# Joining the tokens after layer 0: latents first, with PE doing the sum, and layer 1's queries ahead of the context

## The reference, cut to what matters

```
for l in range(2):
    h = modulate(rms_norm(x, norm1_g), shift, scale)      # the same for ctx with its own shift, scale
    y_lat, y_ctx = parallel_mixer(h_lat, h_ctx, w_in[l], ...)
    x, ctx = x + g1 * y_lat, ctx + cg1 * y_ctx
    f = grouped_moe(concat(h2_ctx, h2_lat), ...)          # per token: w0 * expert_a + w1 * expert_b
    ctx, x = ctx + cg2 * f[:, :256], x + g2 * f[:, 256:]
return rms_norm(x, final_g)                               # layer 1 leaves the context's output out
```

## Time and profile before

| | |
|---|---|
| median of 3 runs | 1466.73 us (1465.39 to 1467.75) |
| profiled execution, first to last instruction | 1467.6 us (the page gives no other time for it) |
| PE busy | 1403.9 us, 96% |
| DVE, ACT, POOL busy | 695.9, 527.6, 157.1 us |
| mean granted clock of TensorE | 0.988 |
| DMA moved | 352.37 MB, mean 240 GB/s |
| PE in slices 23 to 25 (843.9 to 953.9 us) | 8 or 9 tenths and more |

### The profile page before, as it was taken

One profiled execution on the slowest core, in us unless ns is written; L12 is line 12 of the kernel. 1 busy time (PEld: TensorE's weight loads), 2 busy tenths in 40 slices (PEclk: granted clock), 3 DMA queues, 4 the chain that ended last, 5 costly groups with the idle time before them and its releaser, 6 DMA issues. The chain is left out here.

```text
span 1467.6 us, 20788 instructions
## 1 busy us (share of the span) xinstructions
PE 1403.9 (96%) x8454; PEld 899.7 (61%) x8454; DVE 695.9 (47%) x1201; ACT 527.6 (36%) x955; POOL 157.1 (11%) x163
## 2 busy tenths in 40 slices
PE   4999999999999999999999979999998999999997
PEld 2787667646888864444444478876856997344433
DVE  3477986475834442100000035877675864223323
ACT  4554452357233341111111136544346453112112
POOL 0006970000000000000000030074000000000000
PEclk9999999999999999999999989999999999999999
DMA  9862104671131757999999592121577765999994
GB/s 355 250 153 92 53 6 172 229 287 59 58 115 58 286 203 290 374 389 396 402 397 411 226 330 83 58 72 44 200 258 289 284 232 230 387 427 428 427 427 167
DMA packets 102952, 352.37 MB, mean 240 GB/s; under 512 B 23104, under 2 KB 26304, under 8 KB 88000
## 3 DMA queue, kind: packets, MB, share of 16 engines
q1 hardware_dynamic: 99136, 338.09, 60.3%
q0 software_dynamic: 2976, 10.49, 2.1%
q10 hardware_dynamic: 736, 2.36, 0.4%
HBM read 341.48 MB, written 13.63 MB: 242 GB/s over the span
## 5 line engine op out<-in xcount | busy, mean ns | idle before, releaser
L1471 PE MATMUL bank<-narrow_slab,picked 128*64 128x512 f32 x256 | 114.7, 601 | 4.4 <-issue 4.2
L1202 PE MATMUL bank<-slab,feed 128*64 128x512 f32 x512 | 115.8, 605 | 0.2 <-issue 0.2
L1472 PE MATMUL bank<-narrow_slab,picked 128*64 128x512 f32 x256 | 114.7, 601 | 0.0
L864 PE MATMUL bank<-hT,ring 128*128 128x512 f32 (+1 forms) x256 | 102.8, 539 | 0.0
L3101 DVE TENSOR_TENSOR f_acts<-bank,f_silu 64x512 f32<-64x512 f32 x16 | 12.2, 764 | 188.8 <-ACT f_silu L2232 188.8
L1202 PEld LDWEIGHTS bank<-slab,feed 128*64 128x64 f32 x512 | 36.6, 139 | 71.9 <-issue 71.9
L1471 PEld LDWEIGHTS bank<-narrow_slab,picked 128*64 128x64 f32 x256 | 34.1, 138 | 70.2 <-issue 68.8
L2499 POOL DMA_INDIRECT feed_rows<-token_table,slot_token x16 | 14.6, 914 | 555.9 <-DVE slot_token L3033 346.4
L3280 DVE TENSOR_TENSOR hidden<-bank,gated 64x512 f32<-64x512 f32 x16 | 17.4, 1086 | 109.7 <-ACT gated L2374 109.7
L864 PEld LDWEIGHTS bank<-hT,ring 128*128 128x128 f32 x256 | 45.9, 191 | 32.0 <-issue 30.6
L1231 PE MATMUL bank<-slab,f_turned 128*64 128x512 f32 x256 | 58.5, 598 | 0.6 <-issue 0.6
(11 more groups left out here) (421 smaller groups left out, 3025.1 us busy)
## 6 DMA issues: line engine op xcount, KB each, us to landing
ring<-in_w_in SPq DMA_DIRECT2D x23, 2048.0 KB, 11.3
ring<-in_w_ada SPq DMA_DIRECT2D x16, 2048.0 KB, 11.1
slab<-in_w_gate SPq DMA_DIRECT2D x16, 2048.0 KB, 14.8
slab<-in_w_up SPq DMA_DIRECT2D x16, 2048.0 KB, 18.8
slab<-in_w_down SPq DMA_DIRECT2D x16, 2048.0 KB, 19.4
narrow_slab<-in_w_gate SPq DMA_DIRECT2D x16, 2048.0 KB, 15.5
narrow_slab<-in_w_up SPq DMA_DIRECT2D x15, 2048.0 KB, 20.9
narrow_slab<-in_w_down SPq DMA_DIRECT2D x15, 2048.0 KB, 24.6
```

The lines of the kernel that those rows point to most:

```text
L864: mm = T.matmul(beside[0][:, a:TOK], w[:, k, c * P:(c + 1) * P], hT[:, k, a:TOK], start=(k == 0), stop=(k == KT - 1))
L1202: mm = T.matmul(bank[e % 2][NEAR * kind:NEAR * (kind + 1), :], feed[e % 2][:, k, 0:NEAR], w[kind][:, k, :], start=(k == 0), stop=(k == KT ...
L1471: T.matmul(bank[0][0:64, :], x, gate[:, k, :], start=(k == 0), stop=(k == KT - 1))
L1472: mm = T.matmul(bank[0][64:128, :], x, up[:, k, :], start=(k == 0), stop=(k == KT - 1))
```

## The change

The gathers go in the order t = 2, 3, 0, 1 (latents first). The early load of `w_in` block 3 is taken out of its place; SP issues it after the gathers of the first three tiles have landed, and block 4 after the fourth. PE runs 24 idle products in place of 40. A new tile `share_diag` holds for each token tile and each of the two rows a diagonal 128x128 matrix of the shares, made by one multiplication on DVE. PE multiplies the gathered rows by it, so that the scaling, the sum of the two rows and the transposition are one group of 16 products a tile; ACT's scaling, DVE's sum and the transposes go.

The segments are then handled one after the other. PE joins tiles 2, 3 and 0, sums the latents' squares, spreads the latents' factor, and joins tile 1. DVE adds the latents, and then interleaves the latents' norm products with adding the context. PE multiplies the queries by feature tile as soon as the modulated latents are there; behind the third of eight tiles stand the sums of the context's squares, behind the fourth the spread of its factor. The context's squares are made by POOL (five) and DVE (three) in place of ACT, and are not paired. Rounded copies and remainders are made by segment, and the chunks wait for both.

```diff
-        PAIRED = 12
+        JOIN_ORDER = (2, 3, 0, 1)
+        BY_POOL = 5
...
+            def join_squares(sg):
+                key = ("ms", 1, 0) if sg == 0 else ("ms", 1, 0, 1)
+                o = open_bank(key, "norm_std", side=(sg == 0), at=4)
+                for k in range(KT):
...
+                    for t in range(2):
+                        mm = T.matmul(o[:, t:t + 1], square_late[:, KT * sg + k, t * P:(t + 1) * P], ones[:, 0:1],
+                                      start=(k == 0 and t == 0), stop=(k == KT - 1 and t == 1))
...
+            def spread_segment(sg):
...
+                if sg == 1:
+                    idle_products(o[:, 0:P], 2)
+                pe.wait_ge(sem["rstd_found"], stds_before(2) + 2 - sg)
...
+                def join(t):
+                    pe.wait_ge(sem["shares_ready"], 1)
+                    pe.wait_ge(sem[f"tok_there{t}"], 32)
+                    for d in range(KT):
+                        c = d % 2 * SEG + t % 2 * P
+                        for j in range(2):
+                            mm = T.matmul(bank[t // 2 * 4 + d // 2][:, c:c + P], tok_rows[j][:, t, d * P:(d + 1) * P],
+                                          share_diag[:, t, j, :], start=(j == 0), stop=(j == 1))
+                    mm.then_inc(sem["tok_turned"], 1)
...
+                for t in JOIN_ORDER[:3]:
+                    join(t)
+                join_squares(1)
+                spread_segment(1)
+                join(JOIN_ORDER[3])
...
+            def latent_queries():
...
+                for k in range(KT):
+                    pe.wait_ge(sem["h_ready"], normed_before(2) + k + 1)
+                    for c in range(4):
+                        o = bank[6 + c // 2][:, c % 2 * SEG:(c % 2 + 1) * SEG]
+                        mm = T.matmul(o, w[:, k, c * P:(c + 1) * P], hT[:, k, SEG:TOK],
...
+                    if k == 2:
+                        join_squares(0)
+                    if k == 3:
+                        spread_segment(0)
...
-                    idle_products(bank[7][:, P:2 * P], 40)
+                    idle_products(bank[7][:, P:2 * P], 24)
...
-                    fill(first_after[first_lane])
...
-                        for t in range(4):
-                            sp.wait_ge(sem[f"tok_there{t}"], 32)
-                        for s in (4, 5, 6):
+                        for s, before in ((3, JOIN_ORDER[:3]), (4, JOIN_ORDER[3:]), (5, ()), (6, ())):
+                            for t in before:
+                                sp.wait_ge(sem[f"tok_there{t}"], 32)
                             fill(slot_of(("in", 1, s)))
```

ACT in layer 1, where `modulate` over all 512 tokens and the copies behind it stood:

```diff
+                def latents_then_context():
+                    modulate(2, SEG, gain1[:, 1], mod[:, 1, 0:KT, :])
+                    for k in range(KT):
+                        act.wait_ge(sem["h_ready"], normed_before(2) + k + 1)
+                        S.activation(early_hi[:, k, SEG:TOK], hT[:, k, SEG:TOK], ACT.Copy).then_inc(sem["tile_high"], 1)
+                    segment_std(0)
+                    for k in range(KT):
+                        act.wait_ge(sem["normed_ready"], normed_before(2) + KT + k + 1)
+                        S.activation(hT[:, k, 0:SEG], normed[:, k % 2, 0:SEG], ACT.Identity, scale=gain1[:, 1, k, 1:2],
+                                     bias=mod[:, 1, k, 1:2]).then_inc(sem["h_ready"], 1)
+                        act.wait_ge(sem["h_ready"], normed_before(2) + KT + k + 1)
+                        S.activation(early_hi[:, k, 0:SEG], hT[:, k, 0:SEG], ACT.Copy).then_inc(sem["tile_high"], 1)
+                        if k == 3:
+                            near_high(0)
+                    near_high(1)
```

POOL, in place of the pairwise additions of squares:

```diff
+                for k in range(BY_POOL):
+                    if k == 0:
+                        pool.wait_ge(sem["normed_ready"], normed_before(2) + 1)
+                    pool.wait_ge(sem["tok_added"], KT + k + 1)
+                    G.tensor_tensor(square_late[:, k, :], xT[:, k, 0:SEG], xT[:, k, 0:SEG], ALU.mult)\
+                        .then_inc(sem["square_ready"], 1)
```

DVE in layer 1, in place of the norm over all tokens and the remainders behind it:

```diff
+                def latents_then_context():
+                    invert_segment(1)
+                    dve.wait_ge(*is_ready(("rstd", 2)))
+                    rstd = result(("rstd", 2))
+                    for k in range(KT):
+                        if k >= 2:
+                            add_joined(0, k - 2)
+                            dve.wait_ge(sem["h_ready"], normed_before(2) + k - 1)
+                        V.tensor_tensor(normed[:, k % 2, SEG:TOK], xT[:, k, SEG:TOK], rstd[:, SEG:TOK], ALU.mult)\
+                         .then_inc(sem["normed_ready"], 1)
+                    add_joined(0, KT - 2)
+                    add_joined(0, KT - 1)
+                    for k in range(BY_POOL, KT):
+                        dve.wait_ge(sem["tok_added"], KT + k + 1)
+                        V.tensor_tensor(square_late[:, k, :], xT[:, k, 0:SEG], xT[:, k, 0:SEG], ALU.mult)\
+                         .then_inc(sem["square_added"], 1)
+                    for k in range(4):
+                        latent_low(k)
+                    invert_segment(0)
...
+                    for k in range(KT):
...
+                        V.tensor_tensor(normed[:, k % 2, 0:SEG], xT[:, k, 0:SEG], rstd[:, 0:SEG], ALU.mult)\
+                         .then_inc(sem["normed_ready"], 1)
+                        if k < 4:
+                            latent_low(4 + k)
+                        if k:
+                            context_low(k - 1)
+                        if k == 4:
+                            near_low(0)
+                    context_low(KT - 1)
+                    near_low(1)
```

More of the change, by code:

```diff
@@ L288, in build @@
     square_late = fixed("square_late", [P, 2 * KT, SEG], offset=A0)
+    share_diag = fixed("share_diag", [P, 4, 2, P], offset=A0 + 20 * KB)
     hrow = fixed("hrow", [P, 4, D], offset=A0)
@@ L733, in spread_rstd @@
                 o = open_bank(("rstd", count), "rstd_rows")
-                reader["rstd", count] = ("normed_ready", KT * (count + 1))
+                reader["rstd", count] = ("normed_ready", normed_before(count + 1))
                 if count == 1:
@@ new lines, in spread_segment @@
+            def spread_segment(sg):
+                key = ("rstd", 2) if sg == 1 else ("rstd", 2, "context")
+                o = open_bank(key, "rstd_rows", side=(sg == 0), at=5 * sg)
+                reader[key] = ("normed_ready", normed_before(2) + KT * (2 - sg))
+                if sg == 1:
+                    idle_products(o[:, 0:P], 2)
+                pe.wait_ge(sem["rstd_found"], stds_before(2) + 2 - sg)
+                for t in (2 * sg, 2 * sg + 1):
+                    mm = T.matmul(o[:, t * P:(t + 1) * P], token_rstd[:, t:t + 1].to_broadcast([P, P]), ident,
+                                  start=True, stop=True)
+                mm.then_inc(sem[ready[key][2]], 1)
@@ new lines, in join_tokens @@
+            def join_tokens():
+                def join(t):
[7 more added lines that the diff above has]
+                    mm.then_inc(sem["tok_turned"], 1)
+                for b in range(8):
+                    in_bank[b] = ("experts", 0, b)
+                    reader["experts", 0, b] = ("tok_added", 2 * ((b + 4) % 8) + 2)
+                for t in JOIN_ORDER[:3]:
[3 more added lines that the diff above has]
+                join(JOIN_ORDER[3])
@@ L813, in _ @@
                 else:
[L814 to L827 removed]
+                    latent_queries()
                 for n in range(8):
@@ L2622, in add_scaled, with add_joined @@
                 return op
+            def add_joined(sg, d):
+                dve.wait_ge(sem["tok_turned"], 4 - 2 * sg)
+                a = slice(sg * SEG, (sg + 1) * SEG)
+                got = bank[4 * sg + d // 2][:, d % 2 * SEG:(d % 2 + 1) * SEG]
+                V.scalar_tensor_tensor(xT[:, d, a], got, mod[:, 0, 5 * KT + d, 1 - sg:2 - sg],
+                                       xT[:, d, a], ALU.mult, ALU.add).then_inc(sem["tok_added"], 1)
             for l in range(DEPTH):
@@ L2629, in _ @@
                 segs = segs_of[l]
-                if l == 1:
-                    for sg in range(2):
-                        a = slice(2 * sg, 2 * sg + 2)
-                        dve.wait_ge(sem["norm_std"], stds_before(2) + sg + 1)
-                        V.reciprocal(token_rstd[:, a], token_std[:, a]).then_inc(sem["rstd_found"], 1)
                 def tile_low(k):
@@ L2645, in row_low @@
                     V.tensor_tensor(low, w, high[:].bitcast(f32), ALU.subtract).then_inc(sem["way_low"], 1)
-                norm(2 * l, 0, None if l else tile_low)
-                for k in range(KT) if l else (KT - 1,):
-                    tile_low(k)
                 def near_low(n):
@@ L2659, in _ @@
+                if l == 0:
+                    norm(0, 0, tile_low)
+                    tile_low(KT - 1)
+                    near_low(0)
+                    near_low(1)
+                else:
+                    latents_then_context()
```

210 lines of the change are left out of this document (81 added, 129 removed).

## The result

The changed kernel takes 1471.86 us, the median of 9 executions (1468.6 to 1475.55), against 1467.13 (1465.39 to 1469.72) for nine of the kernel before on the same chip: a ratio of 1.0035, 95% interval 1.0026 to 1.0044, slower by 4.7 us. The forecast was 1467.3 with a range up to 1471.0. The profiled execution has a span of 1470.1 us.

The account below looks back on a forecast made before the run. It took PE, busy nearly throughout, to bound the kernel, passing early microseconds on nearly whole. Terms: -2.8 us at full clock, +3.4 for two clock falls, +0.6 in sum, on 1466.73 gives 1467.3 us; range 1462.5 to 1471.

Parts of the forecast that it names:

- POOL's second gather starts at 849.66: Gather step: start time kept from the old timeline, putting the first tile's rows there at 854.2 in place of 857.4.
- 4.5 us for a landing: Gather step: time for a tile's gather to land, within bounds of 4.3 to 7.7 us.
- two short falls of the clock, +3.4: Clock step: two short half-clock stretches at the two runs of sums, 1.7 us each, added to the sum.
- the -2.8: Sum at full clock: the second chunk's first product moves from 901.3 to 898.5 us.
- Rival 3: Gathers don't land earlier, still 857.4; PE waits 3 us, clock may fall before the join; 1470.5 us, chance 0.06.
- Join, sums, last tile, queries: PE's steps: 3.6 us a tile joined, 3.6 per 32 sum passes, 0.22 per query pass, eight passes a token tile.
- Context chain: After the context's spread: ACT's modulate and copy for eight tiles, 10.0 us in all, 884.65 to 894.6; bounds 8.6 to 12.5.
- wide products follow the sums at once: Clock step: reason for taking both falls as the short kind, 3.4 us long and costing 1.7 each.
- Rival 2: Low clock lasts from the latents' sums to the last tile's join: one long, one short fall, +4.0 us; chance 0.16.
- its 11.5 us between 865 and 895: Sign set for the lasting low clock: 11.5 us at half clock in that window would decide for it.
- 1470.7: Time in us forecast if the low clock lasts: -2.8 + 5.1 + 1.7 = +4.0.
- The skill's rule: Clock step: only idle gaps drop the clock; PE has none from 854 to 891, so the sum stays at -2.8.

Follow-up runs that it names:

- e14: Changed kernel with sums moving 128 columns of ones and the last sync-queue store of expert output issued on ACT's queue; 1467.38 us, ratio 0.9996 to before.
- e6: Kernel before with one edit: its sums of squares move 128 equal columns of ones in place of one; 1462.04 us, ratio 0.9967 to before.
- e13: Changed kernel with the last of the sync queue's four closing stores of expert output issued first on ACT's queue; 1471.07 us, ratio 1.0020 to before.
- e12: Second profile of e5, the same program with no edit, this time with the store late; 1468.45 us, ratio 1.0012 to before.
- e5: Changed kernel with one number different: its sums of squares move 128 equal columns of ones in place of one; 1467.92 us, ratio 1.0006 to before.
- e2: Changed kernel with operands of the sums swapped: ones stay in the array, 256 columns of squares move, no spread; 1463.63 us, ratio 0.9979 to before.
- e9: Changed kernel measured again with no edit, for a second profile; 1472.66 us, ratio 1.0039 to before.
- e11: e2 with the old join (ACT scales, DVE adds, PE transposes) and idle products in PE's pauses; 1463.22 us, ratio 0.9982 to before.
- e1: Changed kernel with 40 idle products ahead of the join in place of 24; 1472.43 us, ratio 1.0038 to before.
- e4: Kernel before with only the later w_in load, issued after the gathers of the first three tiles; 1464.95 us, ratio 0.9989 to before.
- e10: Kernel before with the edits of e4 and e6 together: later w_in load and 128 columns of ones; 1461.94 us, ratio 0.9978 to before.

## Why the prediction was wrong

Three terms of the forecast failed, the first most. It let the gathers start as before ("POOL's second gather starts at 849.66"), put nothing down for what has to land ahead of them, and took 4.5 us for a landing that measured 5.1 to 5.8. It took two short falls of the clock, +3.4, where the sums brought a short and a long one, +4.6. The forecast's stage was 51.16 + 3.4 = 54.56 us, and 59.87 came. Of the 5.3 us between, the late store and its fall are 3.3, the falls at the sums 1.2, and the stage at full clock 1.0, mostly the landing; the parts overshoot by 0.2.

The four terms of the loss against the kernel before, each a difference of two stages, with one profile for each:

| term | from | us | forecast |
|---|---|---|---|
| order at full clock | e14 - e6: 52.16 - 50.26 | +1.9 | 51.16 for e14's 52.16 |
| half clock behind the new sums | e13 - e14: 56.78 - 52.16 | +4.6 | +3.4 |
| half clock before, now gone | e6 - before: 50.26 - 53.94 | -3.7 | inside the -2.8 |
| late store and the fall it brings | e12 - e14: 55.47 - 52.16 | +3.3 | none |

The lines of e14 and, second, of e6 from which the stages at full clock are read:

```profile
844.89 7.22 PE L686 MATMUL bank<-const 128*128 128x128 f32 x48 [4.03 <-issue]
...
897.05 2.01 PE L905 MATMUL bank<-early_hi,near_hi 128*128 128x512 f32 x8
```
```profile
846.07 10.80 PE L680 MATMUL bank<-const 128*128 128x128 f32 x80 [4.04 <-issue]
...
896.33 1.98 PE L835 MATMUL bank<-early_hi,near_hi 128*128 128x512 f32 x8
```

The four terms add up to 6.1, and the stages differ by 5.93. With the late store in 6 of 10 executions the mean would be 1.9 + 4.6 - 3.7 + 2.0 = 4.8, near the 4.7 of the medians. That share is counted from profiles and not from the timed executions.

- *The -2.8 at full clock* was nearly right: 51.16 us of stage (847.34 to 898.5) against 52.02 and 52.16. But it set a new kernel at full clock against an old one of which 3.7 us were half clock. At equal clock the order loses 1.9, and e5 beside e6 shows where: the first chunk starts at 44.5 us of the stage in both, since the context's sums and spread (4.3 us) have gone in ahead of it and use up the earlier queries; then it waits for the context's tiles, 7.5 us of products and waits where e6 has 5.7.
- *Gathers.* Landing improved, but less than reckoned. The 4.5 taken is met only by the first gather (4.2 to 4.9 with the weights behind it); the second of a pair is the one to count, 5.1 to 5.8, so the first tile comes 7.5 us into the stage at best (e2, e5) and not 6.9. The step that failed most is "POOL's second gather starts at 849.66", 2.32 us into the stage: in the changed kernel it came at 4.46, and nothing in the forecast asked what else has to land before it.
- *Rival 3* was given 0.06, and its outcome came by another cause: the first pair is there 9.8 us into the stage and not much before the old 10.1, PE waits 2.88 us and the clock falls ahead of the join. But the landing did improve, to 5.3 us; it was the start that was late.
- *Join, sums, last tile, queries.* 3.65 us a tile, 3.63 for 32 passes, 5.34 for three query tiles: as forecast. DVE, ACT and POOL stayed hidden.
- *Context chain.* 10.0 forecast; 9.95 in the changed kernel, from the first context norm product (892.29) to the last tile's high product (902.24).
- *The clock.* Two short falls, +3.4; measured one short and one long, 3.4 and 6.8 us, worth 4.6 (e13, e14). The long one lies under 256-column products (887.64 and 892.04): "wide products follow the sums at once" did not keep it short. Rival 2 named the wrong place for the long fall and the right kind of outcome; its 11.5 us between 865 and 895 were not reached here (10.2) and were in e9 (13.6). That its 1470.7 lies near the result is in part luck, since it holds nothing for the late store.
- *The skill's rule.* By it the sum was to stay at -2.8 for want of gaps. The Trainium skill, "TensorE: Matmul & The Clock Gate", Part 1, has the gate follow how busy PE has been; here PE is busy for 13.60 of 13.60 us and the clock falls, and in e6 it is busy for 8.56 of 10.30 and the clock stays. The measurement decides against the rule as far as busy means instructions in flight.
- *The page of the kernel before.* The slice that holds most of this stage (843.9 to 880.6 us) shows PE at 7 tenths, not at 8 or 9 as the table ahead of the forecast has it; no term of the sum was taken from it. The queries end at 891.7 and not 891.5 by the forecast's own terms, which changes no sum.

Open: whether the new order makes the late store likelier, or the 0 of 4 is chance; with the store in its old place the 16 KB packet begins 1.16 to 1.89 us after the store's issue, and the rows are through at about 1.4. Open too is part of e5's and e14's times: their stages are 1.9 and 1.8 us shorter than before's, their ratios 1.0006 and 0.9996, with 17 and 26 us of half clock after the stage in those profiles. With a late store in six of ten executions (+2.0) the stages give e5 a ratio of 1.0001, and e14, without one, 0.9988. Both lie inside the measured intervals, so these times don't contradict the stages; a small loss behind the stage is not excluded.

## What to carry to other kernels

Bring old and new to the same clock before their stages are subtracted: a gain reckoned against a stretch at half clock belongs to whatever lifts the clock, and here one operand's width gave the kernel before 4 us in its old order. When a transfer is brought forward, look at what still has to land ahead of it, and at what else moves then. Filler paid here where it ended with the wait that it covered (e11), and not where it outlasted it (e1).

## What the runs showed of the hardware

- Thirty-two passes of one column and of 128 columns take the same time here, 3.63 and 3.74 us, but a run of the first had 3.4 to 13.6 us at 1.2 GHz in it or right behind it (before, changed, e1, e4, e9, e13), a run of the second none (e5, e6, e10, e12, e14).
- The last 32 KB store of the sync queue landed in 1.7 to 1.9 us, or in 3.5 to 4.0 where two of its rows started only as a 16 KB instruction packet of 1.3 to 1.6 us ended (six of six late cases).
- A gather of 128 rows of 4 KB landed in 4.2 to 6.9 us (one in 7.5) where the 2 MB load was issued behind the gathers of three tiles, and in 6.9 to 7.7 where it was issued ahead of them (before, e6).
